# A down projection by seven products of operand sums in place of eight, one product at a time

## The reference, cut to what matters

```
x = x + gate1 * (merged @ w_out)
h2 = _rmsnorm(x, norm2_g) * (1 + scale2) + shift2
a, b = jnp.split(h2 @ w_gu, 2, axis=-1)
x = x + gate2 * ((jax.nn.silu(a) * b) @ w_down)
...
y_sample = _rmsnorm(xs, final_g)
```

## Time and profile before

| what | value |
|---|---|
| timed runs | 2016.62, 2015.59, 2012.38 us; median 2015.59 |
| profiled execution, its own time | 2013.09 us |
| profiled execution, span | 2011.3 us, granted TensorE clock 0.987 |
| PE busy | 1940.5 us (96%), 10516 matmuls |
| VectorE, ScalarE, GpSimd busy | 1128.6, 715.2, 700.7 us |
| moved | 247.65 MB, mean 123 GB/s |

### The profile page before, as it was taken

The page is one execution under the profiler, slowest core; times in us unless marked ns, Lnnn a source line. Parts: engine busy times, 40 slices in busy tenths (PEclk is TensorE's granted clock), DMA queues, the critical chain, the costliest instruction groups (busy, mean ns, idle before and its releaser), DMA issues.

```text
span 2011.3 us, 27020 instructions
## 1 busy us (share of the span) xinstructions
PE 1940.5 (96%) x10516; PEld 1706.7 (85%) x10516; DVE 1128.6 (56%) x1852; ACT 715.2 (36%) x1284; POOL 700.7 (35%) x484
## 2 busy tenths in 40 slices
PE   8799999999989999989999999999999999999998
PEld 3799978988988899978888888888888888888898
DVE  5689785166655666427614855554444334453486
ACT  3512232355555555434422332222222222333242
POOL 0000000344443443214451234444444444455465
PEclk9899999999999999989999999999999999999999
DMA  7551333634344442346561132222222215544555
GB/s 304 183 176 50 108 118 131 168 87 98 91 103 96 105 100 62 127 160 198 153 202 67 56 97 89 90 89 69 69 69 69 68 58 198 178 161 170 161 163 185
DMA packets 219024, 247.65 MB, mean 123 GB/s; under 512 B 36753, under 2 KB 169617, under 8 KB 217873
## 3 DMA queue, kind: packets, MB, share of 16 engines
q1 hardware_dynamic: 218896, 245.93, 39.4%
HBM read 185.33 MB, written 60.56 MB: 122 GB/s over the span
## 4 chain that ended last, share of the span: by engine, by line
PE 81%; DVE 9%; DMA 4%; issue 2%; ACT 2%; POOL 1%; SPq 0%; POOLq 0%; DVEq 0%; ACTq 0%
PE ps_all L144 71%; PE ps_all L1050 2%; PE ps_all L1027 2%; PE ps_all L1036 2%; DMA w_raw<-w_in_dram 2%; DVE mod_acc L643 1%; DMA wmod_then_mixers<-w_mod_dram 1%; PE ps_all L445 1%; DMA branch_and_gates<-branch_dram 1%; DVE X L2436 1%; DVE X L2430 1%; DVE AL L2440 1%; DVE softmax_cols L1186 1%; DVE prob L1176 1%; DVE sumsq L2557 0%
## 5 line engine op out<-in xcount | busy, mean ns | idle before, releaser
L144 PE MATMUL ps_all<-AH,w_hi 128*128 128x448 f32 (+3 forms) x1672 | 606.5, 363 | 27.5 <-DVE wmod_then_mixers L652 9.4
L144 PE MATMUL ps_all<-AL,w_hi 128*128 128x448 f32 (+3 forms) x1672 | 593.7, 355 | 0.0
L144 PE MATMUL ps_all<-AH,w_lo 128*128 128x448 f32 (+3 forms) x1672 | 593.3, 355 | 0.0
L144 PEld LDWEIGHTS ps_all<-AH,w_hi 128*128 128x128 f32 x1672 | 319.0, 191 | 57.4 <-DVE wmod_then_mixers L652 9.7
L144 PEld LDWEIGHTS ps_all<-AH,w_lo 128*128 128x128 f32 x1672 | 318.4, 190 | 28.8
L144 PEld LDWEIGHTS ps_all<-AL,w_hi 128*128 128x128 f32 x1672 | 319.4, 191 | 26.3
L2542 DVE TENSOR_TENSOR AL<-hidden_in,AH 128x512 fp32r<-128x512 f32 (+1 forms) x66 | 139.4, 2117 | 137.7 <-ACT AH L2202 137.6
L2504 DVE TENSOR_TENSOR quarter<-ps_all,quarter 128x512 f32<-128x512 f32 x140 | 96.6, 690 | 177.8 <-PE ps_all L144 175.6
L2333 POOL TENSOR_TENSOR slot_lo<-w_pair,slot_hi 128x512 fp32r<-128x512 f32 x96 | 130.4, 1381 | 174.9 <-ACT slot_hi L2172 174.9
L1232 POOL TENSOR_TENSOR w_lo<-w_raw,w_hi 128x1024 fp32r<-128x1024 f32 x21 | 50.3, 2397 | 380.1 <-ACT w_hi L1073 380.1
L144 PE MATMUL ps_all<-AH,slot_hi 128*128 128x256 f32 (+1 forms) x384 | 129.6, 338 | 1.1 <-DVE hidden L2475 1.1
(11 more groups left out here) (231 smaller groups left out, 3744.5 us busy)
## 6 DMA issues: line engine op xcount, KB each, us to landing
w_down_rows<-w_down_dram SPq DMA_DIRECT2D x44, 512.0 KB, 4.1
w_raw<-w_in_dram SPq DMA_DIRECT2D x42, 512.0 KB
wmod_then_mixers<-w_mod_dram SPq DMA_DIRECT2D x20, 1024.0 KB, 8.1
w_pair<-w_gu_dram SPq DMA_DIRECT2D x20, 1024.0 KB, 5.3
hidden<-quarter SPq DMA_DIRECT2D x50, 256.0 KB, 2.1
branch_and_gates<-gates SPq DMA_DIRECT2D x16, 768.0 KB, 4.4
w_raw<-w_down_dram SPq DMA_DIRECT2D x22, 512.0 KB, 3.7
hidden_in<-hidden SPq DMA_DIRECT2D x44, 256.0 KB, 4.0
```

The costliest lines, as they stand in the source:

```text
L144: mm = nc.tensor.matmul(out, w, a[:, k, cols[0]:cols[1]], start=(first and part == 0), stop=(last and part == 2))
```

## The change

The two sample chunks (2 x 2 halves of weights and of hidden values) are multiplied by seven products P1 to P7 of sums of the halves, with 11 inner tiles each, in the order P1, P2, P7, P6, P5, P4, P3; the prompt chunk follows as before with its 22 tiles. A step of a product takes one weight tile of 128 x 512 (256 KB) and one hidden tile of 128 x 512, has four output tiles and so 12 matmuls, and writes half the banks; the next product writes the other half.

Sums are formed on VectorE by a helper `difference` (L2713 of the changed kernel), ahead of the split into high and low parts: weight sums for P1's kept tiles, P6, P5 and P3, token sums for P7, P6, P5 and P4. Eleven weight tiles and eleven hidden tiles that later products share are kept in SBUF (`kept_a`, `kept_b`). In step n of VectorE's queue the sums of n+1 stand ahead of the low part of n. Results of the products are combined on VectorE (L2758, L2774, L2786) and copied by ScalarE into `total1` and `total7`; P4's product is subtracted by a gate of the other sign (`negative_gate`). The squares of finished tiles and their adds stand in P6 and P3 and in the prompt chunk. Raw weights now have six buffers, loaded two steps further ahead; raw hidden tiles still four. `hidden_lower` and the up projection's last multiplication are now written as scalar_tensor_tensor in place of tensor_tensor.

The diff, cut to its core:

```diff
-DOWN = [(c, k) for c in range(3) for k in range(HTILES)]
+HALF_K = HTILES // 2
+DOWN_PRODUCTS = ("P1", "P2", "P7", "P6", "P5", "P4", "P3")
+DOWN = [(name, k) for name in DOWN_PRODUCTS for k in range(HALF_K)] + [("ctx", k) for k in range(HTILES)]
...
+SUM_A, SUM_B = ("P1", "P6", "P5", "P3"), ("P7", "P6", "P5", "P4")
+KEPT_A, KEPT_B = ("P7", "P6"), ("P7", "P6")
+RAW_A, RAW_B = 6, 4
...
             def down_group(n):
...
-                for m in range(KD):
+                for m in range(KD if name == "ctx" else 4):
...
             def load_hidden(n):
...
-                elif n >= 4:
-                    sp.wait_ge(hd_lo, n - 3)
+                elif n >= RAW_B:
+                    sp.wait_ge(hd_lo, n - RAW_B + 1)
...
         def gpsimd(pool):
...
+                name, k = DOWN[n]
+                if name == "P6" and 1 <= k < 5:
+                    final_add(k - 1)
+                elif name == "P3" and 1 <= k < 5:
+                    final_add(4 + k - 1)
+                elif name == "P3" and k >= 8:
+                    final_add(8 + k - 8)
+                elif name == "ctx" and k == 0:
+                    final_add(11)
...
         def vector(dve):
...
+            def difference(out, first, second, sign):
+                return nc.vector.scalar_tensor_tensor(out, first, 1.0, second, ALU.mult, ALU.add if sign > 0 else ALU.subtract)
...
             def hidden_lower(n):
-                w = chunk(DOWN[n][0])
+                hi, lo = token_split(n)
                 dve.wait_ge(hd_hi, n + 1)
-                nc.vector.tensor_tensor(g.AL[:, n % 4, 0:w], hidden_in[:, 4 + n % 4, 0:w], g.AH[:, n % 4, 0:w].bitcast(F32), ALU.subtract).then_inc(hd_lo, 1)
+                difference(lo, token_operand(n), hi.bitcast(F32), -1).then_inc(hd_lo, 1)
...
+            for n in range(len(DOWN)):
+                name, k = DOWN[n]
+                if n + 1 < len(DOWN):
+                    weight_sum(n + 1)
+                    token_sum(n + 1)
                 hidden_lower(n)
+                if name == "P1":
+                    if k >= 2:
+                        kept_weights(k - 2)
+                elif name == "P2":
+                    if k < 2:
+                        kept_weights(HALF_K - 2 + k)
+                elif name == "P7":
+                    if 3 <= k < 7:
+                        evict_p2(k - 3)
+                    elif k >= 7:
+                        finish_11(k - 7)
+                elif name == "P5":
+                    if 3 <= k < 7:
+                        evict_p6(k - 3)
+                elif name == "P4":
+                    if 3 <= k < 7:
+                        evict_p5(k - 3)
+                    elif k >= 7:
+                        finish_22(k - 7)
+                elif name == "P3":
+                    if 3 <= k < 7:
+                        finish_21(k - 3)
+                    elif k >= 7:
+                        begin_12(k - 7)
```

More of the change, by code:

```diff
@@ L1810, in sync @@
                     load_down(0)
+                    load_down(1)
+                    for j in range(2):
+                        load_kept(j)
                 if p % 2 == 1:
@@ L1978, in down_group @@
                     if k == 0:
-                        down_bank_wait(c, m)
-                    if c == 2 and k == 0 and m % 2 == 0:
-                        pe.wait_ge(zeros_ready, 1)
-                        nc.tensor.matmul(g.ps_all[:, m // 2, :], zeros[:, 0:P], zeros[:, :], start=True, stop=False)
-                    half, w = m // 4, slice(m % 4 * P, (m % 4 + 1) * P)
-                    mm = products(nc, down_bank(c, m), hi[:, half, w], lo[:, half, w], g.AH, g.AL, n % 4, (0, chunk(c)),
-                                  k == 0 and c < 2, k == HTILES - 1 and (c < 2 or m % 2 == 1))
@@ L1986, in down_group @@
-                    if k == HTILES - 1:
+                        down_bank_wait(name, m)
+                    if name == "ctx":
+                        if k == 0 and m % 2 == 0:
+                            pe.wait_ge(zeros_ready, 1)
+                            nc.tensor.matmul(g.ps_all[:, 4 + m // 2, :], zeros[:, 0:P], zeros[:, :], start=True, stop=False)
+                        w = (m // 4, slice(m % 4 * P, (m % 4 + 1) * P))
+                        first, last = False, k == HTILES - 1
+                        mm = down_products(down_bank(name, m), hi[:, w[0], w[1]], lo[:, w[0], w[1]], th, tl, first, last and m % 2 == 1)
+                    else:
+                        w = slice(m * P, (m + 1) * P)
+                        first, last = k == 0, k == HALF_K - 1
+                        mm = down_products(down_bank(name, m), hi[:, w], lo[:, w], th, tl, first, last)
@@ L1987, in down_group, with down_products @@
+                    if last:
                         mm.then_inc(m_done, 1)
-                if k < HTILES - 1:
+                if not last:
                     mm.then_inc(k_done, 1)
+            def down_products(out, wh, wl, th, tl, first, last):
+                nc.tensor.matmul(out, wh, th, start=first, stop=False)
+                nc.tensor.matmul(out, wh, tl, start=False, stop=False)
+                return nc.tensor.matmul(out, wl, th, start=False, stop=last)
             def final_wait(job):
@@ L2061, in tensor @@
                 down_group(n)
-                step = n - 2 * HTILES
+                step = n - CTX0
                 if step in (2, 11):
```

402 lines of the change are left out of this document (294 added, 108 removed).

## The result

| | before | after |
|---|---|---|
| median of 17 runs each, us (lowest to highest) | 2015.64 (2012.38 to 2021.74) | 2004.09 (1999.88 to 2012.24) |
| profiled execution, its own time | 2013.09 | 2002.62 |
| span, granted TensorE clock | 2011.3, 0.987 | 2000.8, 0.985 |
| PE busy, matmuls | 1940.5, 10516 | 1920.1, 10384 |
| VectorE, ScalarE, GpSimd busy | 1128.6, 715.2, 700.7 | 1226.3, 740.5, 715.0 |

The change is faster: ratio 0.9941, 95% interval 0.993 to 0.9952, 11.6 us. The forecast was 2006 us and a wait of PE for VectorE and GpSimd in the last four products. Both came. The time of the context part, which the forecast also charged, did not. The fence has the busy time by stage of the kernel after, one row for each stage (that of before for the down projection is the earlier trace rows): P1, P2, P7, P6, P5, P4, P3, the context part, the tail.

What follows compares the result with a forecast made beforehand. PE bound the kernel before; VectorE and GpSimd together would bound the last four products. 2013.1 - 30.0 + 19.2 + 0.5 + 2.0 = 2004.8, plus 1.3 for timed runs: 2006 us, range 1994 to 2019.

Steps and rivals of the forecast that it cites:

- The time of the context part: Context part: starts with no lead, GpSimd's queue still holding P3's last squares; 2 us charged, bounds 0 and 5.
- PE's work: Down projection: 924 matmuls against 1056, at 0.227 us each, 30.0 us less.
- lead: Products: operand preparation runs at most 5.7 us ahead of PE; step time over 2.72 us uses this up first.
- The pair as the bound: P6 to P3: a GpSimd and a VectorE operation together cost 1.70 us; PE waits 19.2 us; chance 0.66.
- case 4: P6 to P3: port lock lasts the whole instruction, 55 GpSimd operations cost 0.27 us more each, 2021 us; chance 0.04.
- the evictions: P5: four PSUM evictions on VectorE at 0.67 us each, not beside GpSimd's operation, 2.7 us.
- P1 to P7 without a gap: Sign of being right: the seven products, 924 matmuls in some 229 us, follow each other without a gap.
- clock 1.00: Sign of being right: PE's granted clock stays at 1.00, the 2.4 GHz level, despite 19.2 us of waiting.
- gaps under 1.5 us: Sign of being right: in P6 to P3 PE's waits on lower parts stay under 1.5 us each, most in P3.
- A clock below 1.00 in P3: Sign of being wrong: PE's granted clock falls below 1.00 in P3.
- case 2: Last four products: waits fall into idle time, PE stays the bound, 30 us come, 1984 to 1989 us; chance 0.14.
- case 3: P7 to P4 and P1: four hidden-tile buffers, landing up to 7.0 us, 3.25 us a step, 2021 us; chance 0.16.

Runs made afterwards that it cites:

- the other form: VectorE's low part written as tensor_tensor in place of scalar_tensor_tensor, against the kernel after; 2004.71 us, ratio to before 0.9948.

## Why the prediction was right, point by point

**PE's work.** 132 matmuls fewer, 30.0 us: right (239.65 - 209.4 = 30.2). The steady distance was 0.227 us, and P2 and P7 took 29.92 us each. P7 used only lead, as said.

**The pair as the bound.** Right, and shown from both sides: shortening GpSimd's half brings P6 to P3 from 17.1 us of waiting to 0.2, VectorE's half to 2.0. The price was right as well: 1.70 us in the rows of P3, and P5's steps stood 2.90 us apart against 2.92. With 1.28 + 0.69 for each pair they would stand 1.97 apart, so case 4 falls. The Trainium skill, "SBUF — State Buffer", section Who interferes with whom, calls the shared ports an exclusive lock, and says of VectorE's 2-port modes that whoever issues first holds them for the whole instruction. That one engine waits, this trace shows (1.77 us for a sum in place of 0.68), and that the wait, 1.09 us, is less than the 1.28 of the whole GpSimd instruction.

**The size.** Terms and measurement, in us beyond 29.92:

| | P1 | P6 | P5 | P4 | P3 | P6 to P3 | context |
|---|---|---|---|---|---|---|---|
| predicted | 0.5 | 2.7 | 4.9 | 3.2 | 8.4 | 19.2 | +2.0 |
| measured | 1.75 | 4.14 | 2.15 | 2.33 | 8.52 | 17.1 | 0.0 |

The sum is 2.1 too high in the four products, 2.0 too high in the context part and 1.3 too low in P1. The start of the down projection, 0.9 later than in the profile of before, was in no term. Together that is the 2.2 us by which the forecast of the profiled execution, 2004.8, was above its 2002.62: part of the errors cancelled, and that was luck.

**The context part.** Its 73.7 us in the kernel before were misread: at 1994.60 the chain goes over to VectorE's eviction of a bank, and PE's matmuls end at 1996.74, so it took 75.8. Nor was it PE's alone: PE waited 0.87 and 1.47 us in it for VectorE's lower part. Ahead of its first step PE waits 1.3 us for GpSimd, counted in P3; inside, the kernel after waits once, 2.36 us, for VectorE behind its adds of squares. P3's own part is then 7.2 us, 1.2 less than forecast, and its agreement with the 8.4 is chance too.

**What was mis-sized.** The lead and the evictions. I let it shrink evenly and put P6's payment at 2.7 and P5's at 4.9; together 7.6, where 6.3 came. In P6 the pairs of the four adds come in a row at its start, PE fell 2.24 us behind in one step, and VectorE then built a lead again while PE ran on at the lower clock. In P5 I had each of the four evictions at 0.67 us, because I put GpSimd's operation beside the sums. They cost nothing: its steps stood 2.90 apart with or without one, until one of 3.40. One of them, VectorE's rows and then GpSimd's:

```profile
1815.95 0.68 DVE L2774 SCALAR_TENSOR_TENSOR w_down_rows<-ps_all,w_down_rows 128x512 f32<-128x512 f32 x1
1816.55 1.17 DVE L2713 SCALAR_TENSOR_TENSOR w_raw<-w_raw,kept 128x512 f32<-128x512 f32 x1
...
1815.56 1.60 POOL L2502 TENSOR_TENSOR w_lo<-w_raw,w_hi 128x512 fp32r<-128x512 f32 x1 [1.29 <-ACT w_hi L2306]
```

The eviction ran beside GpSimd's operation, and the weight sum behind it took 1.17 us where it takes 1.77 in a step without one. P4 was 0.9 too dear.

**What was wrong.** "P1 to P7 without a gap" held, but not "clock 1.00": P1 started at a lowered clock (0.67 between 1684 and 1688 us) and lost 1.6 us. I had called the waits harmless to the clock, and gaps under 1.5 us; they went up to 2.24, and the clock fell behind that one. The forecast of the time survived this, because the only fall among the four products lay where VectorE sets the end (the runs with spread adds and with the other form). My reading of the earlier trace rows by the busy share over 20 us was the failed step: it says nothing of single gaps. A clock below 1.00 in P3, which I had named as a sign of being wrong, came in two profiles of the experiments (0.96) and cost nothing, so it was no sign of that.

**The rivals.** All covered (case 2) did not come, and what it would have given is what the runs that break the pair measured: 1983, against the 1984 to 1989 forecast for it. The ring of hidden tiles (case 3) is refuted by the halved transfers, and in P3, which they left alone, by the run with the short subtraction. Transfers also cost next to nothing in P1: at a share of 0.84 other profiles took 30.02 to 30.04 us there. Of P1's 1.75 us 1.6 are thus the clock, and not the 0.5 that I gave to DMA.

## What to carry to other kernels

When PE's work shrinks per step, price the step anew on VectorE and GpSimd together: count their operations on SBUF operands as pairs that take turns, and look for work that PE, ScalarE or a PSUM operand can take off them. Removing a summation from GpSimd paid only when TensorE did it in wide matmuls; the same sum in narrow ones lost its whole gain. A lowered clock on PE is worth mending only where PE sets the end. And where the end of a stage is read off the chain, look for the engine's last instruction too: the chain may have left it earlier.
